# Recurrent layers' inverse: levels one to four with one group of other products behind the back products, y copied in three parts from three banks

## The reference, cut to what matters

```
pa, pb, pc = split_sizes(h @ w_in[l], (A_PROJ, B_PROJ, C_PROJ))
ya = rwkv7_mixer(pa, ...)      # a recurrence over the tokens, 4 heads of 64
yb = dilated_mixer(pb, ...)    # banded attention, 4 heads
yc = mla_mixer(pc, ...)        # attention over latents, 4 heads
x = x + jnp.concatenate([ya, yb, yc], axis=-1) @ w_out[l]
...
x = x + (jax.nn.silu(h @ w_gate) * (h @ w_up)) @ w_down
```

## Time and profile before

| | |
|---|---|
| runs | 969.14, 969.02, 969.0 us; median 969.02 us |
| profiled execution | 969.5 us, span of its records 967.7 us |
| PE busy | 956.5 us (99%), PEld 865.4 us (89%) |
| DVE, ACT busy | 718.9 us (74%), 544.4 us (56%) |
| granted PE clock | 0.998 of full |
| inverse in the profile, layer one | y products of level 1 at 371.42 us, end of level 5 near 401.5 us; first product of w_out 425.38 us |

### The profile page before, as it was taken

How to read it: one execution, slowest core, us unless ns; L and a number is a source line. 1 busy time by engine, 2 the same in 40 slices (tenths; PEclk the granted TensorE clock), 3 DMA queues, 4 the chain that set the end, 5 groups by cost and what they waited for, 6 DMA issues and landing times.

```text
span 967.7 us, 17457 instructions
## 1 busy us (share of the span) xinstructions
PE 956.5 (99%) x7262; PEld 865.4 (89%) x7262; DVE 718.9 (74%) x1197; ACT 544.4 (56%) x842; POOL 12.6 (1%) x25
## 2 busy tenths in 40 slices
PE   9999999999999999999999999999999999999997
PEld 8999998888888989889988888899888998888886
DVE  6878588787785887867787875567887578877653
ACT  5486566655444783556555553376546456556431
POOL 1000000000000010000000000001000000000000
PEclk9999999999999999999999999999999999999999
DMA  9744445555554332224555555543231356555531
GB/s 342 201 148 180 151 153 202 211 177 185 207 175 169 117 122 89 89 88 148 202 198 207 178 184 207 175 170 128 74 126 45 122 184 210 182 179 209 178 131 44
DMA packets 25142, 156.81 MB, mean 162 GB/s; under 512 B 2896, under 2 KB 4696, under 8 KB 7656
## 3 DMA queue, kind: packets, MB, share of 16 engines
q1 hardware_dynamic: 22320, 151.51, 44.9%
q10 hardware_dynamic: 2072, 2.49, 1.2%
q0 software_dynamic: 672, 1.70, 0.6%
HBM read 153.86 MB, written 1.44 MB: 160 GB/s over the span
## 4 chain that ended last, share of the span: by engine, by line
PE 94%; DVE 2%; issue 1%; ACT 1%; DMA 1%; SPq 0%; DVEq 0%; ACTq 0%
PE bank L527 26%; PE bank L739 21%; PE bank L769 11%; PE bank L744 11%; PE bank L779 6%; PE bank L598 2%; PE bank L773 2%; PE bank L1025 1%; PE bank L603 1%; PE bank L1043 1%; PE bank L1032 1%; PE bank L1280 1%; PE bank L556 1%; PE bank L1255 1%; PE bank L557 1%
## 5 line engine op out<-in xcount | busy, mean ns | idle before, releaser
L1872 DVE TENSOR_TENSOR w_lo<-raw,w_hi 128x2048 fp32r<-128x2048 f32 (+2 forms) x142 | 319.0, 2249 | 106.7 <-ACT w_hi L1313 106.2
L1313 ACT ACTIVATE w_hi<-raw 128x2048 fp32r<-128x2048 f32 (+4 forms) x153 | 273.4, 1788 | 85.7 <-PE bank L779 62.0
L739 PE MATMUL bank<-h_both,w_hi 128*128 128x512 f32 x912 | 217.6, 391 | 0.2 <-DVE arena L1854 0.2
L739 PEld LDWEIGHTS bank<-h_both,w_hi 128*128 128x128 f32 x912 | 167.6, 188 | 32.7 <-issue 0.3
L1313 ACT ACTIVATE arena<-bank 128x256 f32<-128x256 f32 (+3 forms) x189 | 73.8, 403 | 169.7 <-PE bank L744 116.7
L527 PE MATMUL bank<-h_both,w_hi 128*128 128x256 f32 x880 | 164.1, 288 | 0.2 <-DVE w_lo L1872 0.2
L527 PEld LDWEIGHTS bank<-h_both,w_hi 128*128 128x128 f32 x880 | 137.2, 191 | 4.2 <-issue 2.0
L527 PE MATMUL bank<-h_both,w_lo 128*128 128x256 f32 x440 | 124.2, 282 | 0.0
L744 PEld LDWEIGHTS bank<-h_both,w_lo 128*128 128x128 f32 x912 | 116.9, 191 | 4.4
L744 PE MATMUL bank<-h_both,w_lo 128*128 128x256 f32 x912 | 118.3, 283 | 0.0
L769 PE MATMUL bank<-act_both,w_hi 128*128 128x512 f32 x462 | 112.4, 395 | 0.0
(11 more groups left out here) (328 smaller groups left out, 1199.0 us busy)
## 6 DMA issues: line engine op xcount, KB each, us to landing
raw<-in_w SPq DMA_DIRECT2D x136, 1024.0 KB, 4.9
raw<-in_w SPq DMA_DIRECT2D x2, 896.0 KB, 4.5
raw<-in_w SPq DMA_DIRECT2D x3, 512.0 KB, 3.6
raw<-in_w SPq DMA_DIRECT2D x2, 768.0 KB, 4.3
raw<-in_first SPq DMA_DIRECT2D x4, 256.0 KB, 5.5
x<-in_first SPq DMA_DIRECT2D x4, 256.0 KB, 5.7
arena<-bias_rows ACTq DMA_DIRECT2D x4, 256.0 KB, 5.9
cst<-in_consts SPq DMA_DIRECT2D x1, 992.0 KB, 9.6
```

The source lines that it names most:

```text
L739: pe.matmul(to, hi(k), h_both[:, :, k, :], start=(k == 0), stop=False, skip_group_check=True)
L1313: return act.activation(dst, src, ACT.Copy, **kw)
L1872: dve.tensor_tensor(w_lo[:, s, 0:n], raw[:, s, 0:n], w_hi[:, s, 0:n].bitcast(F32), ALU.subtract)\
```

## The change

Four things are done, in both recurrent layers:

- **PE.** The back products of levels 1 to 4 come right behind the y products; what stood between them joins what stood behind. Level 5 stays as it was.
- **Three parts.** The y products of q = 0 are divided: m 0, 1 go to bank 0 and m 2, 3 to bank 2, q = 1 stays in bank 1 (`Y_PARTS`, `y_bank`). ACT copies them in three instructions (128 x 128, 128 x 128, 128 x 256). The back products of q wait for part q + 1.
- **DVE.** x and xt are updated before the other work of the level, not after or amidst it; next y products wait for `inv_xt` directly and the nop (line 2379) goes. latents_lo moves behind level 2's update, `w_lo` of out 0 behind level 4's update, `w_lo` of out 1 from behind probs_of(2, 3) to behind bonus_and_gain, after probs_of(4, 5).
- **ACT.** The latents' rounding (`latents_hi`) and `w_hi` of out 0 come right behind level 2's copies of y; `w_hi` of out 1 moves from the middle of level 3 to behind exponential 3.

```diff
@@ -436,7 +436,11 @@
-        AFTER_LEVEL = {2: ("out", 0)}
+        Y_PARTS = ((0, (0, 1)), (0, (2, 3)), (1, (4, 5, 6, 7)))
+
+        def y_bank(part):
+
+            return quads((0, 2, 1)[part])
@@ -1019,7 +1023,7 @@
                 project(l, 7, between=turn_inverse)
                 def back_products(n):
                     for q in range(2):
-                        pe.wait_ge(A.sem, A.at(l, "inv_y", n, q))
+                        pe.wait_ge(A.sem, A.at(l, "inv_y", n, q + 1))
                         for m in range(4 * q, 4 * q + 4):
                             for h in HALVES:
                                 last = pe.matmul(blocks(quads(2 + q)[h, m % 4, 0:64], n, 1), Y[h, m, :],
@@ -1034,24 +1038,24 @@
                         last.then_inc(M.sem, M.mark(l, "inv_z", n, q))
 
                 for n in range(1, 6):
-                    for q in range(2):
-
-                        pe.wait_ge(V.sem, V.at(l, "inv_bt", n, q))
-                        pe.wait_ge(A.sem, A.at(l, "inv0", q)) if n == 1 else pe.wait_ge(V.sem, V.at(l, "inv_x", n - 1, q))
-                        for m in range(4 * q, 4 * q + 4):
+                    for part, (q, ms) in enumerate(Y_PARTS):
+                        if part != 1:
+                            pe.wait_ge(V.sem, V.at(l, "inv_bt", n, q))
+                            pe.wait_ge(A.sem, A.at(l, "inv0", q)) if n == 1 else \
+                                pe.wait_ge(V.sem, V.at(l, "inv_xt", n - 1, q))
+                        for m in ms:
                             for h in HALVES:
-                                last = pe.matmul(quads(q)[h, m % 4, 0:64], BT[h, m, :], Xm[h, m, :],
+                                last = pe.matmul(y_bank(part)[h, m % 4, 0:64], BT[h, m, :], Xm[h, m, :],
                                                  start=True, stop=True)
-                        last.then_inc(M.sem, M.mark(l, "inv_y", n, q))
+                        last.then_inc(M.sem, M.mark(l, "inv_y", n, part))
+                    if n == 5:
+                        beside_inverse(l, n, 0)
+                    back_products(n)
                     if n == 1:
-                        project(l, 8, between=lambda: back_products(1))
-                        continue
-                    beside_inverse(l, n, 0)
-                    back_products(n)
-                    if n == 5:
-
-                        break
-                    beside_inverse(l, n, 1)
+                        project(l, 8)
+                    elif n < 5:
+                        beside_inverse(l, n, 0)
+                        beside_inverse(l, n, 1)
@@ -1600,17 +1604,12 @@
                             act.wait_ge(V.sem, V.at(l, "in", 6 + n))
                             act.wait_ge(M.sem, M.at(l, "gram", 7))
                             copy(to[:, 0, :], flat(src)).then_inc(A.sem, A.mark(l, "swap", n))
-                        act.wait_ge(M.sem, M.at(l, "in", 8))
-                        act.wait_ge(V.sem, V.at(l, "c_n"))
-                        copy(cq_hi[:, 0:2, :], b["cqn"])
-                        copy(cq_hi[:, 2, :], b["ckvn"]).then_inc(A.sem, A.mark(l, "c_hi"))
                     for i in {2: (0, 1), 3: (2, 3), 4: (4,)}.get(n, ()):
                         up(i)
                         if i == 2:
                             act.wait_ge(M.sem, M.at(l, "b_rot"))
                             act.wait_ge(A.sem, A.at(l, "up", 2))
                             copy(swap_q[:, 0, :], flat(b["qr"])).then_inc(A.sem, A.mark(l, "swap", 2))
-                            hi_of(CHUNK[l, "out", 1])
                     if n == 5:
                         exponential(l, 0)
                         right_side(0, 0)
@@ -1618,17 +1617,25 @@
                         up(5)
                         up(6)
 
+                def latents_hi():
+                    act.wait_ge(M.sem, M.at(l, "in", 8))
+                    act.wait_ge(V.sem, V.at(l, "c_n"))
+                    copy(cq_hi[:, 0:2, :], b["cqn"])
+                    copy(cq_hi[:, 2, :], b["ckvn"]).then_inc(A.sem, A.mark(l, "c_hi"))
+
                 def up(i):
                     act.wait_ge(M.sem, M.at(l, "up", i))
                     act.activation(up_to[i], up_bank(i), ACT.Copy, scale=scale if i < 3 else 1.0)\
                         .then_inc(A.sem, A.mark(l, "up", i))
 
-                def inverse_y(n, q):
-                    act.wait_ge(M.sem, M.at(l, "inv_y", n, q))
+                def inverse_y(n, part):
+                    q, ms = Y_PARTS[part]
+                    act.wait_ge(M.sem, M.at(l, "inv_y", n, part))
                     if n >= 2:
                         act.wait_ge(M.sem, M.at(l, "inv_z", n - 1, q))
-                    copy(Y[:, 4 * q:4 * q + 4, :], quads(q)[:, :, 0:64])\
-                        .then_inc(A.sem, A.mark(l, "inv_y", n, q))
+                    first, end = ms[0], ms[-1] + 1
+                    copy(Y[:, first:end, :], y_bank(part)[:, first % 4:first % 4 + len(ms), 0:64])\
+                        .then_inc(A.sem, A.mark(l, "inv_y", n, part))
 
@@ -1724,11 +1731,12 @@
                     act.wait_ge(M.sem, M.at(l, "inv0", q))
                     copy(Xm[:, 4 * q:4 * q + 4, :], quads(q)[:, :, 0:64]).then_inc(A.sem, A.mark(l, "inv0", q))
                 for n in range(1, 6):
-                    for q in range(2):
-                        inverse_y(n, q)
+                    for part in range(3):
+                        inverse_y(n, part)
+                    if n == 2:
+                        latents_hi()
+                        hi_of(CHUNK[l, "out", 0])
                     beside_inverse(n)
-                    if n in AFTER_LEVEL:
-                        hi_of(CHUNK[l, *AFTER_LEVEL[n]])
 
@@ -1739,6 +1747,7 @@
                 turned(l, 1)
                 exponential(l, 2)
                 exponential(l, 3)
+                hi_of(CHUNK[l, "out", 1])
                 turned(l, 2)
                 turned(l, 3)
                 exponential(l, 4)
@@ -2230,8 +2239,8 @@
                             after_a(l, "swap", i)
                             tt(to[:, 1, :], flat(src), to[:, 0, :].bitcast(F32), ALU.subtract, l, "swap_rest", i)
                         evacuate(l, 8, B2["bv"], token_major=True)
+                    if (n, half) == (2, 0):
                         latents_lo()
-                    if (n, half) == (2, 0):
                         after_m(l, "b_rot")
                         rotate(0, B2["bq"], B2["bq"], pairs(6), 0)
                     if (n, half) == (2, 1):
@@ -2248,6 +2257,7 @@
                     if (n, half) == (4, 0):
                         lo_of(CHUNK[l, "out", 0])
                     if (n, half) == (4, 1):
+                        after_v(l, "rotated", 2)
                         after_a(l, "up", 2)
                         after_m(l, "q_rot")
                         rotate(3, b["qr"], b["qr"], pairs(7), 2)
@@ -2360,9 +2370,10 @@
                 for n in range(1, 6):
                     if n < 5:
                         for q in range(2):
-                            after_m(l, "inv_y", n, q)
+                            after_m(l, "inv_y", n, q + 1)
                             level(n + 1, q, BT).then_inc(V.sem, V.mark(l, "inv_bt", n + 1, q))
-                    beside_inverse(n, 0)
+                    if n == 5:
+                        beside_inverse(n, 0)
                     for q in range(2):
                         if n < 5:
                             after_m(l, "inv_z", n, q)
@@ -2370,20 +2381,18 @@
                                 after_a(l, "inv0", q)
                             tt(*(blocks(v, n, 0) for v in (q4(Xm, q), q4(Xm, q), quads(q)[:, :, 0:64])), ALU.subtract,
                                l, "inv_x0", n, q)
-                        after_m(l, "inv_zt", n, q)
+                        else:
+                            after_m(l, "inv_zt", n, q)
                         tt(*(blocks(v, n, 1) for v in (q4(XT, q), q4(XT, q), quads(2 + q)[:, :, 0:64])),
                            ALU.subtract, l, "inv_xt", n, q)
-                        if n == 5:
-                            continue
-                        dve.wait_ge(V.sem, V.at(l, "inv_xt", n, q))
-                        dve.nop().then_inc(V.sem, V.mark(l, "inv_x", n, q))
+                    if n < 5:
+                        beside_inverse(n, 0)
                     beside_inverse(n, 1)
 
                 negated(0, 0)
                 logits_of(2, 3)
                 negated(0, 1)
                 probs_of(2, 3)
-                lo_of(CHUNK[l, "out", 1])
                 logits_of(4, 5)
                 after_m(l, "s1")
                 after_a(l, "ex")
@@ -2393,6 +2402,7 @@
                 probs_of(4, 5)
                 bonus_and_gain()
+                lo_of(CHUNK[l, "out", 1])
                 mix_lo_of(2, pairs(6), (l, "b_hi"), l, "b_lo")
                 logits_of(6, 7)
                 negated(1, 0)
```

## The result

The changed kernel took 971.93 us (median of 7), the kernel before 969.14 us beside it (7): a ratio of 1.0033, interval 1.0023 to 1.0042. The profiled execution took 971.63 us, with a span of 969.9.

What follows compares the result with a forecast made beforehand. PE, busy 99% of the span, bounds the kernel, so time falls only if its instructions start closer together. Layers of +1.55 and +1.36 us give +2.9 us over the median of 969.02: 971.9 us, range 969.0 to 973.9.

Steps and rivals of the forecast that it cites:

- Joined products: PE, levels 1 to 4: tile-shape changes saved between y and back products, -0.33 us a place, -1.32 us a layer.
- Wait for the copies: Levels 1 and 2: PE waits for ACT's copies of y before the back products, +0.11 us in each.
- Level 2, latents: DVE does x and xt before the latents, so `up` 0 stalls 0.55 us instead of 0.06: +0.49 us.
- Level 3: ACT's copy of `up` 1 delays the copies of y, +0.14 us, an old wait of 0.12 goes: +0.02 us.
- Level 4: On ACT, `up` 2, swap_q and `up` 3 stand before the copies of y, so back products wait: +0.66 us.
- Level 5 and take_off(0): `w_lo` of out 0 makes logits late, take_off(0) stalls 0.58 us: +0.45 us in the first layer, +0.26 in the second.
- `w_lo` of out 1: Its new place on DVE makes negated(1, 0) late, so take_off(1) and the transposes wait: +1.05 us a layer.
- rival of the hidden `w_lo`: ACT frees `turned` and exponential 4 earlier, so out 1's late `w_lo` costs nearly nothing: 969.8 us, chance 0.14.
- dearer shape changes: Tile-shape changes on PE cost more than counted, a joined place saves 0.6 us: 969.7 us, chance 0.09.
- waits hidden under products: Eight stalls a layer lose up to 0.45 us each to running products: 967.0 us; hidden by less, chance 0.05.
- more queues slipping: Small copies don't overlap and ACT's or DVE's lag passes on, 0.3 us at eight places: 974.3 us, chance 0.09.

Runs made afterwards that it cites:

- e10: e6 with three added products of 128 x 128 by 128 x 256 in level 1, one between each two groups of back products; 969.18 us.
- e11: e6 with the same three added products in level 1 as e10, all together behind the back products; 967.29 us.
- e4: The changed kernel with latents_lo on DVE moved ahead of level 2's update of x and xt; 971.45 us.
- e3: The changed kernel with swap_q's copy on ACT moved from between `up` 2 and 3 to behind level 4's copies of y; 972.02 us.
- e5: e2 with `w_lo` of out 0 also moved, from behind level 4's update to behind logits_of(4, 5); 0.9994 of the kernel before.
- e1: The changed kernel with `w_lo` of out 1 moved from behind bonus_and_gain to directly behind logits_of(4, 5); 969.69 us.
- e2: The changed kernel with `w_lo` of out 1 moved from behind bonus_and_gain to directly ahead of `w_lo` of out 2; 969.67 us.
- e6: The changed kernel with the moves of e3, e4 and e5 together, `w_lo` of out 1 late as in e2; 966.76 us.
- e8: e6 with PE's order of before in levels 1 to 4, one group of other products between y and back products; 974.69 us.
- e12: e6 with `w_lo` of out 1 back behind bonus_and_gain; 972.62 us.
- e7: e6 with y copied in two parts from two banks, as before the change, instead of three; 967.28 us.
- e9: The changed kernel run once more, unaltered, for more executions; 971.80 us.

## Why the prediction was right

Predicted 971.9, measured 971.93 us. An agreement to 0.03 is partly luck, as medians of the same kernel differ by some tenths from one set of executions to the next; what the runs bear out are the steps. Per layer:

- *Joined products*, -0.33 a place: 0.31 measured (e10, e11). The Trainium skill, "TensorEngine Tiling (Array Packing)", section Key Properties, says that changing the tiling mode drains TensorE. The trace agrees in part only, as the earlier trace rows had it: in e10 the next group starts 0.07 before the row of the one ahead ends (372.47 for 372.54, 372.78 for 372.85; the ends are modelled). Had it waited for both ends, a round trip would cost 0.45 by these rows (an estimate), not 0.31.
- *Wait for the copies*, +0.11: back products at y + 1.06 (1.05 predicted), y1-y2 at -0.21 (-0.33 + 0.11 = -0.22).
- *Level 2, latents*: `up` 0 at y + 4.63 (4.62 predicted); the interval +0.30, where -0.33 + 0.11 + 0.49 = +0.27. e4 shows the cause. Taking the latents away gave 0.67: the stall of 0.55 as predicted, which the +0.49 counts from the 0.06 of before, and the restart of some 0.1 that before had as well.
- *Level 3*: -0.29 (-0.31), but by two slips that cancel. The prediction had the back products at y + 1.17 and counted the stall from 1.03 (+0.14); they came at y + 1.09, and as the y products are issued by 0.94, the stall is 0.15. From 0.94 its own 1.17 would have given 0.23, and -0.22 for the level.
- *Level 4*: back products at y + 1.58 (1.60), the interval +0.31 (+0.33); e3 shows the cause.
- *Level 5 and take_off(0)*: logits at y5 + 3.39 (3.38), but +0.32 instead of +0.45, and +0.12 instead of +0.26 in the second layer. The stall was over-sized, 0.58 where e5 gives 0.43. The logits came 0.7 later after y5, as predicted, but negated(0, 0) only 0.59 later (6.90 for 6.31): it started 0.30 behind the operation ahead of it before (404.37 and 404.67) and 0.19 now (404.65 and 404.84), so 0.11 of the lateness was taken in there. e5 shows the cause.
- *`w_lo` of out 1*, +1.05: 0.74 to take_off(1) and 0.27 behind it, 1.01. e1 and e2 show the cause.

To w_out the sum is +1.44 and +1.23 (predicted 1.55 and 1.36), 2.67 us in all for the predicted 2.9; the medians say 2.79. Between w_out of the first layer and y of the second nothing changed (269.76 and 269.79). The rival of the hidden `w_lo` falls with e1, that of dearer shape changes with e10 and e11, that of waits hidden under products with e5 and e6, where each wait taken away gave its time back, and that of more queues slipping with the intervals y1 to y5, which sum to +0.11 over before (predicted +0.05). Not foreseen was the clock: some executions of this kernel lie 1.7 to 2.0 us higher. Profiles of executions in which the clock fell were taken of e3, e8 and e12 only; for this kernel that cause is read across from them, not shown.

## What to carry to other kernels

Joining groups of products of one tile shape saves a fixed 0.31 us a place here, of which the copies that are no longer covered take back some 0.1 (0.22 was left in level 1), and the other engines' helpers must then be placed anew: of 1.44 us a layer lost, all and more came from four helper operations that stood in front of what PE waits for. Put a long helper where its engine would wait anyway, and only as many as that idle time holds: one `w_lo` of 2.28 us in VectorE's idle time cost nothing (e1, e5). The one behind bonus_and_gain cost 0.85 to take_off(1) alone (e1 against the changed kernel), and 1.34 with another already in that idle time (e12). A pause of PE may be paid twice (that its clock falls for it is argued here, not shown), so look at the spread of executions and the clock before you read a median as no gain.

## What the runs showed of the hardware that was not expected

**The clock behind a pause.** Seven of the experiments have no PE wait at take_off(1) and none over 0.45 us in the inverse. In six of them (e1, e2, e5, e6, e7, e11) the 63 executions stay, kernel by kernel, within 1.5 us. With a wait of 0.78 there, 3 of 12 (changed kernel), 6 of 9 (e3) and 4 of 8 (e4) executions are 1.5 us or more longer than the others, and 7 of 9 (e12, with 1.27) are 0.67 us or more longer. So are 4 of 5 of e8, whose longest wait is 1.13. e3's profile has the clock at 0.50 from 422.5 to 425.5, e12's from 745.5 to 751.5, e8's from 711 to 714; PE had gone on behind its wait at 420.08, 743.99 and 710.32. A pause is not enough by itself: the same waits stand in the other layer of each of these three profiles, and in both layers of the changed kernel's, e4's and e9's, with the clock at 1.00. Nor does it seem to be needed: the seventh of these kernels, e10, has four longer executions at a lower mean clock, and the profile of one of its shorter ones shows no such wait. So the pause and the lower clock go together here, but that one causes the other is not shown, and which executions it takes stays open.

**VectorE beside GpSimd.** An add of 128 x 256 took 1.37 us in the changed kernel, where it runs beside GpSimd's subtraction (both start within 0.3 us), and 0.42 before, where that was over. The changed kernel's VectorE and GpSimd, then VectorE before:

```profile
394.07 1.37 DVE L1863 TENSOR_TENSOR spare<-spare 128x256 f32<-128x256 f32 x1
```

```profile
393.79 1.37 POOL L514 TENSOR_TENSOR swap_q<-spare,swap_q 128x512 fp32r<-128x512 f32 x1 [46.87 <-ACT swap_q L1317]
```

```profile
394.43 0.42 DVE L1854 TENSOR_TENSOR spare<-spare 128x256 f32<-128x256 f32 x1
```

The add ends at 395.44, 0.28 after GpSimd's end at 395.16 (spans on GpSimd are rough). The Trainium skill, "SBUF — State Buffer", section Who interferes with whom, says that a VectorE instruction with two SBUF inputs contends with a GpSimd instruction that reads SBUF; the trace agrees, with 0.95 us lost. PE lost nothing by it: VectorE still waits 0.17 for PE before its last update of this level, at 396.68.
